# The last weights in pieces, the residual as a matmul, and a last layer norm on three engines

## The reference, cut to what matters

```python
# y: the tokens (256, 1024) after the second block's first layer norm, x in the code
logits = y @ router_w + router_b
top_val, top_idx = top_k(logits, 4)          # of 32 experts
gates = softmax(top_val)
# for every expert e, on the tokens that chose it:
gt = minimum(xb @ w_gate[e] + b_gate[e], 7)
up = clip(xb @ w_up[e] + b_up[e], -7, 7)
ys = (gt * sigmoid(1.702 * gt) * (up + 1)) @ w_down[e] + b_down[e]
out = sum over a token's four experts of gate * ys
x = layer_norm(2 ** 0.25 * y + out, ln2_g, ln2_b)   # mean, variance, eps 1e-5, times g, plus b
```

## Time and profile before

| | us |
|---|---|
| median of 3 runs | 2372.69 |
| lowest and highest | 2370.49, 2373.14 |
| the profiled execution | 2368.61 |
| its span | 2366.8 |
| TensorE busy in the span | 2180.9 (92%) |
| DVE busy | 868.8 (37%) |
| ScalarE busy | 561.8 (24%) |
| GpSimd busy | 28.5 (1%) |

### The profile page before, as it was taken

One profiled execution on the slowest core, in us unless ns is written; L12 is line 12 of the kernel. 1 busy time (PEld: TensorE's weight loads), 2 busy tenths in 40 slices (PEclk: granted clock), 3 DMA queues, 4 the chain that ended last, 5 costly groups with the idle time before them and its releaser, 6 DMA issues.

```text
span 2366.8 us, 27091 instructions
## 1 busy us (share of the span) xinstructions
PE 2180.9 (92%) x11610; PEld 1446.4 (61%) x11610; DVE 868.8 (37%) x1529; ACT 561.8 (24%) x923; POOL 28.5 (1%) x61
## 2 busy tenths in 40 slices
PE   6998999999899999999999879999988998998996
PEld 3766887878676578999887763333333333333332
DVE  4344443442683756754365621111111111111113
ACT  3222332241432435544333420000000000000000
POOL 0000000000001200000000000000000000000000
PEclk7999999999999999999999988999999999999999
DMA  9443343422422444555421549999999999999995
GB/s 347 178 143 107 107 142 116 146 79 104 142 92 85 152 170 143 182 168 183 165 90 37 214 162 418 395 429 427 428 427 428 429 427 428 428 428 428 428 428 213
DMA packets 156333, 594.03 MB, mean 251 GB/s; under 512 B 6288, under 2 KB 78096, under 8 KB 130992
## 3 DMA queue, kind: packets, MB, share of 16 engines
q1 hardware_dynamic: 154208, 589.66, 62.9%
q10 hardware_dynamic: 2000, 2.57, 0.4%
HBM read 591.16 MB, written 1.05 MB: 250 GB/s over the span
## 4 chain that ended last, share of the span: by engine, by line
PE 77%; DMA 13%; DVE 6%; ACT 3%; issue 1%; SPq 1%; ACTq 0%; POOL 0%; DVEq 0%; POOLq 0%
PE ps L887 21%; PE ps L275 13%; PE ps L276 13%; PE ps L277 13%; DMA ring<-in_w_up_dram 11%; PE ps L856 3%; PE ps L873 2%; DVE wr L994 2%; PE ps L357 2%; PE ps L612 1%; PE ps L591 1%; DMA ring<-in_even_w_in_dram 1%; PE ps L598 1%; SPq L2025 1%; PE ps L371 1%
## 5 line engine op out<-in xcount | busy, mean ns | idle before, releaser
L887 PE MATMUL ps<-ring,big 128*64 128x512 f32 x3072 | 694.7, 608 | 80.2 <-DMA ring<-in_w_up_dram 51.3
L887 PEld LDWEIGHTS ps<-ring,big 128*64 128x64 f32 x3072 | 249.8, 140 | 496.3 <-issue 484.7
L275 PE MATMUL ps<-h_hi,wr 128*128 128x512 f32 (+1 forms) x960 | 340.8, 355 | 29.3 <-DVE h_lo L1046 25.1
L994 DVE TENSOR_TENSOR wr<-ring,wr 128x1024 fp32r<-128x1024 f32 (+1 forms) x248 | 283.6, 1202 | 134.9 <-ACT wr L1612 134.8
L276 PE MATMUL ps<-h_lo,wr 128*128 128x512 f32 (+1 forms) x960 | 332.8, 347 | 0.0
L277 PE MATMUL ps<-h_hi,wr 128*128 128x512 f32 (+1 forms) x960 | 332.6, 346 | 0.0
L1612 ACT CAST wr<-ring 128x1024 fp32r<-128x1024 f32 (+1 forms) x248 | 238.6, 1031 | 127.6 <-PE ps L277 96.3
L275 PEld LDWEIGHTS ps<-h_hi,wr 128*128 128x128 f32 x960 | 184.7, 192 | 61.5 <-issue 34.7
L276 PEld LDWEIGHTS ps<-h_lo,wr 128*128 128x128 f32 x960 | 184.8, 193 | 23.5 <-issue 2.9
L277 PEld LDWEIGHTS ps<-h_hi,wr 128*128 128x128 f32 x960 | 184.4, 192 | 22.0
L1461 DVE TENSOR_SCALAR hT<-ps 128x512 f32<-128x512 f32 x32 | 20.6, 686 | 256.3 <-PE ps L913 256.3
(11 more groups left out here) (293 smaller groups left out, 2685.3 us busy)
## 6 DMA issues: line engine op xcount, KB each, us to landing
ring<-in_w_gate_dram SPq DMA_DIRECT2D x64, 2048.0 KB, 22.1
ring<-in_w_up_dram SPq DMA_DIRECT2D x64, 2048.0 KB, 18.3
ring<-in_w_down_dram SPq DMA_DIRECT2D x64, 2048.0 KB, 22.3
ring<-in_ada_w_dram SPq DMA_DIRECT2D x24, 2048.0 KB, 10.9
ring<-in_ffn_w_up_dram SPq DMA_DIRECT2D x44, 1024.0 KB, 7.6
ring<-in_ffn_w_down_dram SPq DMA_DIRECT2D x16, 1408.0 KB, 6.1
ring<-in_w_in_dram SPq DMA_DIRECT2D x9, 2048.0 KB, 7.9
ring<-in_odd_w_qkv_dram SPq DMA_DIRECT2D x6, 2048.0 KB, 8.1
```

The costliest lines, as they stand in the source:

```text
L275: e.matmul(o, l[0], r[0], start=first, stop=False)
L887: ins = e.matmul(pts[hf][HALF[z], :], lhs[:, k, HALF[z]], wt[:, k % 4, 512 * hf:512 * hf + 512], start=k == 0, stop=False, skip_group_chec ...
L994: e.tensor_tensor(wr[:, x], ring[:, x], h.bitcast(F32), SUB).then_inc(s_wlo, 1)
```

## The change

1. **Pieces.** The last pair's loads of up half 1, down half 0 and down half 1 (u = 186 to 191) are replaced by pieces of one or two row groups k for each of both experts (`PIECES`), each with a semaphore of its own that both experts' transfers raise. SP issues them at the odd u, so behind the waits for both slots. `both` waits for a piece at the k where it begins. `landed_expert` counts the slots' semaphores without them, for the conditional pairs.
2. **Scatter.** `scatter(14)` moves from its place between up and down weights of pair 15 into the middle of that pair's down weights (`between`, after k = 3). The last scatter (`last_scatter`) goes by token half: both matmuls of half 0, then both of half 1, each half raising `s_fin`. It waits for both halves of y first.
3. **Residual.** DVE writes alpha times the identity (`alphaI`) ahead of the first gates, and the ledger adds four matmuls, alphaI against the turned yN, into the accumulating banks. The DVE additions at the end go.
4. **Layer norm.** DVE takes the statistics from PSUM, ScalarE computes (x - mean) / sigma from PSUM to SBUF, and DVE and GpSimd share the multiplication by g and the addition of b: GpSimd has columns 512 to 1023 of token half 0 and 768 to 1023 of half 1, DVE the rest.

```diff
+    alphaI = nc.alloc_sbuf_tensor_at("alphaI", [P, P], F32, offset=b_wk + 4 * 1024)
...
+    LAST = 12 * (NE // 2 - 1)
+    PIECES = [(LAST + 6, 0, 2), (LAST + 6, 2, 3), (LAST + 6, 3, 4), (LAST + 8, 0, 2), (LAST + 8, 2, 4),
+              (LAST + 10, 0, 2), (LAST + 10, 2, 3), (LAST + 10, 3, 4)]
+    in_pieces = {u + z for u, _, _ in PIECES for z in range(2)}
+
+    def landed_expert(u):
+
+        return s_w[u % 7], 16 * sum(x not in in_pieces for x in range(u % 7, u + 1, 7))
...
+        def last_scatter(b):
+
+            for n in range(2):
+                e.wait_ge(*emptied(("y", b, n)))
+            for q in range(2):
+                for n in range(2):
+                    ins = e.matmul(ps[2 * q + n][:, :], SgT[turn_of(b)][:, P * q:P * q + P], ySB[turn_of(b)][:, n, :], start=False,
+                                   stop=False, skip_group_check=True)
+                ins.then_inc(s_fin)
+
-        def both(pts, lhs, u, first):
+        def both(pts, lhs, u, first, between=None):
...
-                if k % 4 == 0:
+                if k % 4 == 0 and v not in in_pieces:
                     for z in range(2):
-                        e.wait_ge(s_w[(v + z) % 7], 16 * ((v + z) // 7 + 1))
+                        e.wait_ge(*landed_expert(v + z))
+                for i, (x, k0, _) in enumerate(PIECES):
+                    if (x, k0) == (v, k % 4):
+                        e.wait_ge(s_piece[i], 32)
...
+                if k == 3 and between:
+                    between()
...
-            if 0 < b < NE // 2:
+            if 0 < b < NE // 2 - 1:
                 scatter(b - 1)
...
-            both(pts, HT[turn_of(b)], u + 8, ("y", b, 0))
+            both(pts, HT[turn_of(b)], u + 8, ("y", b, 0), (lambda: scatter(b - 1)) if b == NE // 2 - 1 else None)
...
+            e.wait_ge(s_alpha, 1)
             for n in range(2):
                 for i in range(2):
-                    pt = take(e, ("acc", n, i), bank=2 * n + i, by=(s_fin, 1))
+                    pt = take(e, ("acc", n, i), bank=2 * n + i, by=(s_fin, n + 1))
                     e.matmul(pt[:, :], GT[:, P * n:P * n + P], bdn[:, 512 * i:512 * i + 512], start=True, stop=False,
                              skip_group_check=True)
+                    e.matmul(pt[:, :].rearrange("p (q k) -> p q k", k=KC), alphaI[:, :],
+                             turned(yN[:, n, :])[:, 64 * i:64 * i + 64, :], start=False, stop=False, skip_group_check=True)
...
-        scatter(NE // 2 - 1)
-        e.matmul(ps[7][0:1, 0:1], ones[:, 0:1], ones[:, 0:1], start=True, stop=True,
-                 skip_group_check=True).then_inc(s_fin)
+        e.wait_ge(*emptied(("sgt", NE // 2 - 1)))
+        last_scatter(NE // 2 - 1)
...
+        e.tensor_scalar(alphaI[:, :], ident, ALPHA, None, MULT).then_inc(s_alpha, 1)
...
+        def spread(n):
+
+            e.wait_ge(s_troot, n + 1)
+            at = tail(e.reciprocal(sm[n][:, 1:2], sm[n][:, 0:1]))
+            e.wait_ge(*at)
+            e.wait_ge(*aggr_at[n])
+            spread_at[n] = tail(e.tensor_scalar(sm[n][:, 2:3], mv[n][:, 0:1], sm[n][:, 1:2], -1.0, MULT, MULT))
+
         for n in range(2):
+            e.wait_ge(s_fin, n + 1)
             for i in range(2):
-                z = zN[:, n, 512 * i:512 * i + 512]
-                at = tail(e.scalar_tensor_tensor(z.rearrange("p (q k) -> p q k", k=KC),
-                                                 turned(yN[:, n, :])[:, 64 * i:64 * i + 64, :], ALPHA,
-                                                 accs[n][i][:, :].rearrange("p (q k) -> p q k", k=KC), MULT, ADD))
-                e.wait_ge(*at)
-                at = tail(e.bn_stats(bst[n][:, i, :], z))
+                at = tail(e.bn_stats(bst[n][:, i, :], accs[n][i][:, :]))
+                if n == 1 and i == 0:
+                    spread(0)
...
+        for m, (n, c0, c1) in enumerate(((0, 0, 512), (1, 0, 512), (1, 512, 768))):
+            if m == 1:
+                spread(1)
+            z = zN[:, n, c0:c1]
+            e.wait_ge(s_xhat, (1, 3, 4)[m])
+            at = tail(e.tensor_tensor(z, z, l2g[:, c0:c1], MULT))
             e.wait_ge(*at)
...
+            out_at[m] = tail(e.tensor_tensor(z, z, l2b[:, c0:c1], ADD))
...
+            e.wait_ge(*spread_at[n])
+            for i in range(2):
+                e.activation(zN[:, n, 512 * i:512 * i + 512], accs[n][i][:, :], ACT.Identity, bias=sm[n][:, 2:3],
+                             scale=sm[n][:, 1:2]).then_inc(s_xhat, 1)
...
+        for m, (n, c0, c1) in enumerate(((0, 512, 1024), (1, 768, 1024))):
+            z = zN[:, n, c0:c1]
+            e.wait_ge(s_xhat, 2 * m + 2)
+            e.tensor_tensor(z, z, l2g[:, c0:c1], MULT).then_inc(s_ptail, 1)
+            e.wait_ge(s_ptail, 2 * m + 1)
+            e.tensor_tensor(z, z, l2b[:, c0:c1], ADD).then_inc(s_ptail, 1)
...
-            e.dma_start(view(ring, SLOT * XS[u % 7], SLOT), src[2 * (u // 12) + z].rearrange(
-                "(p k) n -> p (k n)", k=KC)[:, SLOT * hf:SLOT * hf + SLOT]).then_inc(s_w[u % 7], 16)
+            if u not in in_pieces:
+                e.dma_start(view(ring, SLOT * XS[u % 7], SLOT), src[2 * (u // 12) + z].rearrange(
+                    "(p k) n -> p (k n)", k=KC)[:, SLOT * hf:SLOT * hf + SLOT]).then_inc(s_w[u % 7], 16)
+            if u in in_pieces and z == 1:
+                for i, (x, k0, k1) in enumerate(PIECES):
+                    for y in range(2 * (x == u - 1)):
+                        e.dma_start(view(ring, SLOT * XS[(x + y) % 7], SLOT)[:, D * k0:D * k1], src[
+                            2 * (u // 12) + y].rearrange("(p k) n -> p (k n)", k=KC)[
+                            :, SLOT * hf + D * k0:SLOT * hf + D * k1]).then_inc(s_piece[i], 16)
```

More of the change, by code:

```diff
@@ L167, in build @@
     s_fin, s_tail, s_troot, s_out = sem("s_fin"), sem("s_tail"), sem("s_tail_root"), sem("s_out")
+    s_alpha, s_xhat, s_ptail = sem("s_alpha"), sem("s_tail_normed"), sem("s_tail_pool")
+    s_piece = [sem(f"s_last_pair{i}") for i in range(8)]
     def cols_of(w, c0, n):
@@ L1571, in tail @@
             return s_tail, tails[0]
-        e.wait_ge(s_fin, 1)
         bst = [wk[n][:, 0:12].rearrange("p (i s) -> p i s", i=2) for n in range(2)]
         mv = [wk[n][:, 16:18] for n in range(2)]
+        def spread(n):
[4 more added lines that the diff above has]
+            spread_at[n] = tail(e.tensor_scalar(sm[n][:, 2:3], mv[n][:, 0:1], sm[n][:, 1:2], -1.0, MULT, MULT))
@@ L1584, in dve @@
             e.wait_ge(*at)
             aggr_at[n] = tail(e.bn_aggr(mv[n], bst[n]))
-        for n in range(2):
-            e.wait_ge(s_troot, n + 1)
-            e.wait_ge(*aggr_at[n])
-            at = tail(e.reciprocal(sm[n][:, 1:2], sm[n][:, 0:1]))
-            e.wait_ge(*at)
-            if n == 0:
-                e.wait_ge(s_late2[1], 16)
-                e.wait_ge(s_late2[2], 16)
-            for i in range(2):
-                z, cs = zN[:, n, 512 * i:512 * i + 512], slice(512 * i, 512 * i + 512)
-                at = tail(e.scalar_tensor_tensor(z, z, mv[n][:, 0:1], l2g[:, cs], SUB, MULT))
-                e.wait_ge(*at)
-                out_at[n, i] = tail(e.scalar_tensor_tensor(z, z, sm[n][:, 1:2], l2b[:, cs], MULT, ADD))
@@ L1600, in build @@
-    aggr_at, out_at = {}, {}
+        e.wait_ge(s_late2[1], 16)
+        e.wait_ge(s_late2[2], 16)
+        for m, (n, c0, c1) in enumerate(((0, 0, 512), (1, 0, 512), (1, 512, 768))):
[4 more added lines that the diff above has]
+            at = tail(e.tensor_tensor(z, z, l2g[:, c0:c1], MULT))
+            e.wait_ge(*at)
+            out_at[m] = tail(e.tensor_tensor(z, z, l2b[:, c0:c1], ADD))
+    aggr_at, spread_at, out_at = {}, {}, {}
@@ L2111, in sync @@
                         "o (p k) n -> p (o k) n", k=KC)[:, 4 * hf:4 * hf + 4, :]).then_inc(s_w[u % 7], 16)
-        for n in range(2):
-            for i in range(2):
-                cs = slice(512 * i, 512 * i + 512)
-                e.wait_ge(*out_at[n, i])
-                e.dma_start(out[P * n:P * n + P, cs], zN[:, n, cs]).then_inc(s_out, 16)
+        for n, i, at in ((0, 0, [out_at[0]]), (0, 1, [(s_ptail, 2)]), (1, 0, [out_at[1]]), (1, 1, [out_at[2], (s_ptail, 4)])):
+            cs = slice(512 * i, 512 * i + 512)
+            for x in at:
+                e.wait_ge(*x)
+            e.dma_start(out[P * n:P * n + P, cs], zN[:, n, cs]).then_inc(s_out, 16)
         e.wait_ge(s_out, 64)
```

## The result

| | before | after |
|---|---|---|
| median, same chip, 11 runs each (us) | 2369.20 | 2376.03 |
| ratio | | 1.003, 95% interval [1.002, 1.004] |
| profiled execution: time / span (us) | 2368.61 / 2366.8 | 2373.95 / 2372.2 |

The changed kernel is slower by 6.8 us, more than the 4.7 that the prediction took as the least to be told from no change. The forecast was 2372.7, no change, with a range of 2367.5 to 2380.5. The time lies in the range, but two of the three terms were sized too low in cost and the third too high in gain, and the base of 2372.7 was 3.5 above the median of 2369.20 of the kernel before. "Slower" had 0.27.

What follows compares the result with a forecast made beforehand. TensorE was taken to bound the kernel through the ledger, the weight stream afterwards. Ledger +6.3, last pair +0.1 and tail -6.4 sum to 0.0 on a base of 2372.7, forecasting 2372.7 us, range 2367.5 to 2380.5.

Steps and rivals of the forecast that it cites:

- the base of 2372.7: Whole kernel: starting time for the forecast, put on the median of the runs shown, 2372.69 us.
- What bounds the kernel: Ledger: TensorE binds there, the weight stream afterwards, so time added to TensorE in the ledger moves everything behind it.
- The ledger, +6.3: Ahead of pair 1's gate weights: four added residual matmuls, eight records at 0.78 us for the turned read, cost 6.3 us.
- Rival A: Ledger: turned operand fetched fresh for each pass, 12.5 instead of 6.3 us, giving 2378.9; chance 0.20.
- Rival D: Ledger: clock recovers and turned read is free, 0.9 to 3.4 us instead of 6.3, giving 2367.3 to 2369.8; chance 0.16.
- The last pair, +0.1: Last pair: wait of 2.70 gone, 0.9 gained before the transposes, scatter adds 3.65; sum +0.1 us, bounds -0.9 to +1.8.
- (b): Last pair, before the transposes: without pair 14's scatter there, they follow DVE directly, gaining 0.9 us.
- (c): Last pair, middle of the down weights: the moved scatter finds no wait to fill and adds 3.65 us.
- rival C: Last pair: clock falls once more as TensorE idles behind the up weights, +1.7 us, 2374.4; chance 0.27 shared with B.
- The tail, -6.4: After the last down weights (E): span ends at E + 13.5 instead of 19.95, saving 6.4 us.
- Rival B: Tail: DVE and GpSimd cannot read at once, about E + 13.8 instead of 11.1, +2.7 us; chance 0.27 shared with C.
- the row of 868 ns: Tail, evidence against B: longest GpSimd instruction 868 ns against a median of 682, not a whole instruction more.

Runs made afterwards that it cites:

- The grouped order: Changed kernel with the ledger's four old matmuls first, then the four residual ones, instead of alternating; one run, 2371.19 us.
- the straight read: Changed kernel with residual matmuls reading contiguous columns instead of turned ones, timing only; one run 2369.51 us, then six runs 2374.83 us, 1.0031 of before.
- the kernels that avoid the meeting: Changed kernel, residual in pairs 2 to 5, and either no GpSimd in the layer norm (one run, 2365.01 us) or VectorE reading PSUM (one run, 2371.95).

## Why the prediction was right or wrong

**What bounds the kernel.** Right. The residual alone lengthened the ledger by 8.9, the restart of the stream by 7.9 and the time by 7.4; the same matmuls in pairs 2 to 5 cost nothing.

**The ledger, +6.3; measured +7.9.** The term was mis-sized. It was worked out from VectorE's turned reads, 0.78 a record "nearly whatever the clock is". The grouped order shows such a price, 0.86 at either clock, so the idea was sound; but it is not what sets the cost here, as the straight read took the same 2.00 us per matmul at 0.50. What sets it is the other price that stood beside it: 0.85 a record at 1.2 GHz, eight records 6.8, and 2.1 for the alternation of 32-row and full-height matmuls (2.00 instead of 1.71, seven times), which no term had, since before has no such alternation; less 1.07 that the records behind the ledger give back. That return was given as a lower bound, up to 2.5, and left out of the value taken. Rival A fell: no record took 1.4 or more. Rival D came half true in one execution only: there the clock stayed up and the ledger cost 0.9 at the restart, but its read was straight, and six runs of that kernel have the slow median. A turned read is not free with the clock up.

**The last pair, +0.1; measured +3.3.** The step that failed is (b) and (c), the moved scatter. Its own arithmetic held: 3.70 in the middle, 0.8 gained ahead of the transposes (they start 3.42 behind the start of the bias instead of 4.20), the wait of 2.70 gone. But the scatter in its old place was cover for the clock as well, and the sum put that at nothing. With the hole of 2.69 in its place the clock fell, and the down weights' first half lost 1.5 to 1.8, in all eight such executions: rival C, which I gave as +1.7 and counted as a side case. The other 1.7, in the up weights, follows no edit and was lost by seven of thirteen executions; why is open. The bounds, -0.9 to +1.8, left no room for both.

**The tail, -6.4; measured -4.0.** Rival B, +2.7 and E + 13.8, is what happened: E + 13.46. Of the 2.4 missing, 2.2 lie between DVE's first multiplication and its last addition, 7.0 instead of 4.8; the kernels that avoid the meeting got back 1.1 to 1.7 of them. The statistics started at E + 3.1 instead of E + 2.6, but the first multiplication came only 0.1 late. The Trainium skill, SBUF — State Buffer, section SBUF: two separate sides, states that a GpSimd read and a VectorE instruction with two SBUF inputs lock each other out. The trace agrees (1.79 for 0.69, and 0.72 unchanged with one input in PSUM). I set the row of 868 ns against it; in its trace no VectorE instruction with two input tensors in SBUF runs beside line L2002, so it was no evidence.

**The sum.** Each of the three errors lay on the same side: +1.6, +3.2 and +2.4, together 7.2. The time missed the forecast by only 3.3 because the base, taken from a median of three runs, was 3.5 too high: the median of eleven is 2369.20. That the number came out so near is luck in that part. The change itself, +6.8 against 0.0, is inside the range whichever of the two bases is taken. Two small readings were off as well, without weight: 3.70 us for eight records is 0.46 each by division, 0.43 from start to start; and D's low end is 2367.3, not 2367.5.

## What to carry to other kernels

Where a transfer stream stands still because an engine doesn't free its slots, time added on that engine goes to the end (here +7.9 at the restart, +7.4 in the time); a few pairs later, where it waits for the stream, the same work was free. Before moving work away from a place where TensorE would otherwise idle, ask what TensorE then does there: the clock can fall in or behind the hole, and that is paid in the matmuls that follow. A single execution whose clock differs from the others is no measurement of the edit: look at the granted clock first, and repeat.

## What the runs showed of the hardware that was not expected

- An f32 matmul of 512 columns whose moving operand steps 128 elements took 1.90 us alone at 2.4 GHz and 1.73 in a row at either clock (0.86 a record); a straight one took 1.05 at 2.4 GHz among the alternating ones. At 1.2 GHz, alternating, both took 2.00.
- Alternating 32-row and 128-row matmuls took 2.00 us each at 1.2 GHz, those in a row of their own kind 1.71 and 1.73.
- In twelve of thirteen executions the clock fell to 0.50 some 0.9 to 1.0 us after the start of the ledger's first 512-column matmul, behind TensorE's short waits for ScalarE. In the changed kernel it stayed there for 14 us in which TensorE was busy without a gap; in the grouped one it was at 1.00 again from 1473.5 to 1475.4. Why one kept its clock is open.
- A VectorE instruction with two SBUF inputs beside GpSimd took 1.26 to 1.79 instead of 0.69, and sharing the work took longer (7.00) than doing all of it on VectorE (5.72).
